# The second MLP product of 24 of 32 hidden row tiles as Strassen's seven products, in three groups

## The reference

```python
def finish_layer(x, pool_out, attn_out, w_out, ln2, w_ff1, w_ff2):
    h = x + jnp.einsum('bte,ed->btd', jnp.concatenate([pool_out, attn_out], axis=-1), w_out)
    a = jnp.square(jax.nn.relu(jnp.einsum('btd,df->btf', rmsnorm(h, ln2), w_ff1)))
    return h + jnp.einsum('btf,fd->btd', a, w_ff2)
```

## Time and profile before

| | us |
|---|---|
| median of three runs | 1344.92 |
| the profiled execution: span from first to last instruction | 1342.0 |
| up product, Strassen part (669.70 to 952.18) | 282.48 |
| down, group 0 (952.18 to 998.60) | 46.42 |
| down, groups 1 to 6 (998.60 to 1278.50) | 279.90 |
| last group and final norm (1278.50 to 1342.0) | 63.50 |

### The profile page before, as it was taken

The page is one execution under the profiler, slowest core; times in us unless marked ns, Lnnn a source line. Parts: engine busy times, 40 slices in busy tenths (PEclk is TensorE's granted clock), DMA queues, the critical chain, the costliest instruction groups (busy, mean ns, idle before and its releaser), DMA issues.

```text
span 1342.0 us, 25249 instructions
## 1 busy us (share of the span) xinstructions
PE 1308.6 (98%) x9720; PEld 1213.7 (90%) x9720; DVE 695.1 (52%) x1613; ACT 533.7 (40%) x1077; POOL 583.8 (44%) x607
## 2 busy tenths in 40 slices
PE   5999999999999999999999999999999999999998
PEld 4959999995667899779999999999999999999997
DVE  6368998759974222137843443433634334433445
ACT  6445888638766222235533333333310110011034
POOL 5434984432330312221476767767333333333610
PEclk9999999999999999999999999999999999999999
DMA  6430124210010966872332332323521333133203
GB/s 194 93 90 16 48 56 123 86 32 1 2 33 17 325 209 190 269 238 80 104 128 89 121 104 97 120 94 110 206 100 45 112 113 112 47 113 112 63 1 130
DMA packets 143550, 141.69 MB, mean 106 GB/s; under 512 B 21080, under 2 KB 111320, under 8 KB 143423
## 3 DMA queue, kind: packets, MB, share of 16 engines
q1 hardware_dynamic: 124933, 116.31, 27.3%
q10 hardware_dynamic: 17842, 21.94, 4.5%
q0 software_dynamic: 656, 1.84, 0.6%
HBM read 111.87 MB, written 26.50 MB: 103 GB/s over the span
## 4 chain that ended last, share of the span: by engine, by line
PE 84%; DVE 4%; ACT 2%; issue 1%; DMA 0%; SPq 0%; DVEq 0%; ACTq 0%
PE bank L2102 77%; PE bank L2293 3%; PE bank L2392 2%; DVE junk L1675 1%; PE bank L2347 1%; ACT sjunk L1123 1%; PE bank L2150 1%; DVE cc_lo L1755 0%; DVE hid_lo L2027 0%; PE bank L2634 0%; DVE lack L1679 0%; PE bank L2319 0%; DVE prob L1768 0%; DVE hn_lo L1903 0%; ACT prob L1215 0%
## 5 line engine op out<-in xcount | busy, mean ns | idle before, releaser
L2102 PE MATMUL bank<-hid_hi,w_hi 128*128 128x384 f32 (+1 forms) x672 | 217.6, 324 | 0.0
L2102 PE MATMUL bank<-hid_lo,w_hi 128*128 128x384 f32 (+1 forms) x672 | 216.1, 324 | 0.8 <-DVE hid_lo L2027 0.8
L2102 PE MATMUL bank<-hid_hi,w_lo 128*128 128x384 f32 (+1 forms) x672 | 216.2, 322 | 0.0
L2059 DVE TENSOR_TENSOR acc<-bank,acc 128x384 f32<-128x384 f32 x168 | 87.7, 524 | 199.3 <-PE bank L2102 199.3
L693 POOL TENSOR_TENSOR w_hi<-w_raw,zero 128x256 fp32r<-128x256 f32 x108 | 68.5, 634 | 202.3 <-PE bank L2102 186.0
L907 POOL TENSOR_TENSOR w_hi<-w_raw,zero 128x1024 fp32r<-128x1024 f32 x29 | 54.9, 1893 | 221.3 <-PE bank L2102 203.4
L2102 PE MATMUL bank<-xn_hi,w_hi 128*128 128x384 f32 (+1 forms) x456 | 150.6, 330 | 0.0
L2102 PE MATMUL bank<-xn_lo,w_hi 128*128 128x384 f32 (+1 forms) x456 | 147.3, 323 | 0.0
L2102 PE MATMUL bank<-xn_hi,w_lo 128*128 128x384 f32 (+1 forms) x456 | 146.9, 322 | 0.0
L1420 ACT ACTIVATE hid_hi<-hraw 128x1056 fp32r<-128x1056 f32 x32 | 32.7, 1077 | 256.2 <-PE bank L2102 167.1
L2102 PE MATMUL bank<-hi_T,hn_hi 128*128 128x264 f32 x448 | 127.5, 285 | 0.0
(11 more groups left out here) (300 smaller groups left out, 3213.0 us busy)
## 6 DMA issues: line engine op xcount, KB each, us to landing
w_raw<-in_w_ff_dram SPq DMA_DIRECT2D x50, 512.0 KB, 3.5
hraw<-hidden_dram SPq DMA_DIRECT2D x16, 1056.0 KB, 7.5
page<-in_cache_k_dram SPq DMA_DIRECT2D x64, 256.0 KB, 3.6
page<-in_cache_v_dram SPq DMA_DIRECT2D x64, 256.0 KB, 3.4
hidden_dram<-stg ACTq DMA_DIRECT2D x56, 264.0 KB, 2.0
w_raw<-in_w_in_dram SPq DMA_DIRECT2D x18, 512.0 KB, 3.6
wr<-in_w_ff_dram SPq DMA_DIRECT2D x14, 512.0 KB, 4.6
xrow<-in_x_prompt_dram SPq DMA_DIRECT2D x8, 512.0 KB, 8.1
```

Source lines behind the costliest of these rows:

```text
L2059: nc.vector.tensor_tensor(v, ps[:, 0:w], v, ALU.add).then_inc(freeof(("dn", gi, m, g)), 1)
L2102: return nc.tensor.matmul(out, lhsT, rhs, start=start, stop=stop)
```

## The change

Groups 0 and 7 stay as they are. The 24 hidden tiles between them, groups 1 to 6, become SG = 3 groups of eight tiles. In each, the product (1024 output features x 1024 hidden rows) by (1024 hidden rows x 1056 tokens) is cut in half in all three directions: `a11`, `a12`, `a21`, `a22` are quarters of the weights (first index: half of the output features, second: half of the hidden rows; 4 x 512 = 2048 elements per partition), `b11` to `b22` quarters of the hidden rows (first index: half of the rows, second: half of the tokens; 4 x 528 = 2112 elements). Seven products are formed, in the order P1, P2, P5, P3, P6, P7, P4, each of four row blocks by two runs of 264 columns by four tiles of K by three matmuls, 96 matmuls in all.

For each product ScalarE copies the a operand and then the b operand to `ao_hi` and `bo_hi` (two slots each, so a copy waits for the product before the last), GpSimd subtracts to get `ao_lo`, VectorE to get `bo_lo`. In place, GpSimd forms four sums of the a quarters and VectorE four of the b quarters in each group. SP loads the quarters, each as soon as its place has been used for the last time.

The products are summed over the three groups: P2 to P5 go straight into quarters of `acc`, P1, P6 and P7 into SBUF tiles of their own. Only in the third group, between its products, does VectorE combine them (`combine_parts`, 8 kinds x 4 row blocks, 528 elements each). The low half of the last hidden rows (`last_low`) is formed within the third group's P4, and the last weights are loaded to places of their own and split by ScalarE and GpSimd at the end of it.

```diff
+    KH = 4
+    SG = (DFF // P - 2 * FG) // (2 * KH)
+    DPRODS = ["P1", "P2", "P5", "P3", "P6", "P7", "P4"]
+    NQ = 7 * SG
+    MP = KC // 2
+    NCF = 8 * MP
...
+        b_q = {n: at(n, A_X + j * BQ, [P, KH, HT], F) for j, n in enumerate(("b11", "b21", "b12", "b22"))}
+        a_q = {n: at(n, o, [P, KH, MP * P], F) for n, o in (("a11", A_X + 6 * BQ), ("a22", A_X + 6 * BQ + AQ),
+                                                          ("a12", A_V + 2 * HS), ("a21", A_V + 2 * HS + AQ))}
...
+        bo_hi = [at(f"bo_hi{i}", o, [P, KH, HT], R) for i, o in enumerate((A_X + 4 * BQ, A_V))]
+        bo_lo = [at(f"bo_lo{i}", o + BQ, [P, KH, HT], R) for i, o in enumerate((A_X + 4 * BQ, A_V))]
+        ao_hi = [at(f"ao_hi{i}", o, [P, KH, MP * P], R) for i, o in enumerate((A_O0, A_O1))]
+        ao_lo = [at(f"ao_lo{i}", o + AQ, [P, KH, MP * P], R) for i, o in enumerate((A_O0, A_O1))]
...
+        for q in range(NQ):
+            for i in range(MP):
+                for h in range(2):
+                    take(("ds", q, i, h), 2 * ((MP * q + i + 3) % 4) + h)
...
+            def a_load(sg, n):
+                m, h = int(n[1]) - 1, int(n[2]) - 1
+                f0 = FG + 2 * KH * sg + KH * h
+                sp.dma_start(a_q[n][:, :, :], wf2k[:, f0:f0 + KH, MP * P * m:MP * P * (m + 1)]).then_inc(s_qa[n], 16)
+
+            def b_load(sg, n):
+                h, t = int(n[1]) - 1, int(n[2]) - 1
+                f0 = FG + 2 * KH * sg + KH * h
+                sp.dma_start(b_q[n][:, :, :],
+                             hid_d[f0:f0 + KH, :, HT * t:HT * (t + 1)].rearrange("k p t -> p k t")).then_inc(s_qb[n], 16)
...
-            for gi in range(NG):
-                for i in range(FG):
-                    down_load(gi, i, N_FF + FG + FG * gi, 0)
-                    if gi == 0 and i == 1:
-                        hidden_load(0)
-                    if i == 2 and gi + 1 < NG:
-                        hidden_load(gi + 1)
...
+                    stored_upto(FG + 2 * KH)
+                    for s in range(2):
+                        wait_full(sp, ("P3", NPR - 1, s))
+                    b_load(0, "b11")
+                    a_load(0, "a11")
+            b_load(0, "b12")
+            b_load(0, "b21")
+            a_load(0, "a22")
+            sp.wait_ge(s_fl, FG)
+            a_load(0, "a12")
+            a_load(0, "a21")
+            b_load(0, "b22")
+            for sg in range(1, SG):
+                q0 = 7 * (sg - 1)
+                stored_upto(FG + 2 * KH * (sg + 1))
+                sp.wait_ge(s_dbs, 4 * (sg - 1) + 2)
+                b_load(sg, "b12")
+                sp.wait_ge(s_dal, q0 + 4)
+                a_load(sg, "a12")
+                sp.wait_ge(s_dal, q0 + 5)
+                sp.wait_ge(s_das, 4 * (sg - 1) + 4)
+                a_load(sg, "a21")
+                sp.wait_ge(s_dbl, q0 + 5)
+                sp.wait_ge(s_dbs, 4 * (sg - 1) + 4)
+                b_load(sg, "b22")
+                sp.wait_ge(s_dal, q0 + 6)
+                a_load(sg, "a11")
+                sp.wait_ge(s_dbl, q0 + 6)
+                b_load(sg, "b11")
+                sp.wait_ge(s_dbl, q0 + 7)
+                b_load(sg, "b21")
+                sp.wait_ge(s_dal, q0 + 7)
+                a_load(sg, "a22")
...
+            sp.wait_ge(s_dbs, 4 * (SG - 1) + 2)
+            hidden_in(hlast, DFF // P - FG, 0, s_hd[2])
+            sp.wait_ge(s_dal, q0 + 4)
+            for i in range(2):
+                sp.dma_start(wl_raw[i][:, :].rearrange("p (k n) -> p k n", k=FG), wf2[NG - 1, i]).then_inc(s_lw, 16)
+            sp.wait_ge(s_dal, q0 + 5)
+            sp.wait_ge(s_das, 4 * (SG - 1) + 4)
+            for i in range(2, FG):
+                sp.dma_start(wl_raw[i][:, :].rearrange("p (k n) -> p k n", k=FG), wf2[NG - 1, i]).then_inc(s_lw, 16)
+            sp.wait_ge(s_dbl, q0 + 5)
+            sp.wait_ge(s_dbs, 4 * (SG - 1) + 4)
+            hidden_in(hlast, DFF // P - FG, 2, s_hd[3])
...
+            def a_low(q, n):
+                pool.wait_ge(s_dah, q + 1)
+                nc.gpsimd.tensor_tensor(ao_lo[q % 2][:, :, :], a_q[n][:, :, :], ao_hi[q % 2][:, :, :].bitcast(F),
+                                        ALU.subtract).then_inc(s_dal, 1)
+
+            def a_sum(dst, x, y, op):
+                nc.gpsimd.tensor_tensor(a_q[dst][:, :, :], a_q[x][:, :, :], a_q[y][:, :, :], op).then_inc(s_das, 1)
+
+            for sg in range(SG):
+                q0 = 7 * sg
+                a_low(q0, "a11")
+                a_low(q0 + 1, "a12")
+                pool.wait_ge(s_qa["a21"], Q_LOADED + 16 * (sg + 1))
+                pool.wait_ge(s_qa["a22"], Q_LOADED + 16 * (sg + 1))
+                a_sum("a21", "a21", "a22", ALU.add)
+                a_low(q0 + 2, "a21")
+                pool.wait_ge(s_das, 4 * sg + 1)
+                pool.wait_ge(s_dal, q0 + 3)
+                a_sum("a21", "a21", "a11", ALU.subtract)
+                pool.wait_ge(s_das, 4 * sg + 2)
+                a_sum("a12", "a12", "a21", ALU.subtract)
+                a_low(q0 + 3, "a12")
+                a_sum("a11", "a22", "a21", ALU.subtract)
+                a_low(q0 + 4, "a21")
+                a_low(q0 + 5, "a11")
+                a_low(q0 + 6, "a22")
+            for i in range(FG):
+                pool.wait_ge(s_wha, len(act_high) + i + 1)
+                nc.gpsimd.tensor_tensor(wl_lo[i][:, :], wl_raw[i][:, :], wl_hi[i][:, :].bitcast(F),
                                         ALU.subtract).then_inc(s_wlo, 1)
-            wait_full(pool, ("dn", NG - 2, KC - 1, 2))
+            pool.wait_ge(s_cf, NCF)
...
+            def product_high(q):
+
+                sg, name = q // 7, DPRODS[q % 7]
+                if q == 0:
                     act.wait_ge(s_fl, FG)
+                elif q == 1:
+                    wait_full(act, ("dn", 0, KC - 1, 2))
                 else:
-                    wait_full(act, ("dn", gi - 2, KC - 1, 2))
-                for k in ks:
-                    act.wait_ge(s_hd[2 * slot + k // 2], 16 * (gi // 2 + 1))
-                    nc.scalar.activation(hid_hi[slot][:, k, :], src[:, k, :], ACT.Copy).then_inc(s_hh, 1)
+                    wait_full(act, ("ds", q - 2, MP - 1, 1))
+                a, a_steps = {"P1": ("a11", 0), "P2": ("a12", 0), "P5": ("a21", 1), "P3": ("a12", 3), "P6": ("a21", 2),
+                              "P7": ("a11", 4), "P4": ("a22", 0)}[name]
+                b, b_steps = {"P1": ("b11", 0), "P2": ("b21", 0), "P5": ("b12", 1), "P3": ("b22", 0), "P6": ("b22", 2),
+                              "P7": ("b11", 3), "P4": ("b21", 4)}[name]
+                if a_steps:
+                    act.wait_ge(s_das, 4 * sg + a_steps)
+                else:
+                    act.wait_ge(s_qa[a], Q_LOADED + 16 * (sg + 1))
+                nc.scalar.activation(ao_hi[q % 2][:, :, :], a_q[a][:, :, :], ACT.Copy).then_inc(s_dah, 1)
+                if b_steps:
+                    act.wait_ge(s_dbs, 4 * sg + b_steps)
+                else:
+                    act.wait_ge(s_qb[b], Q_LOADED + 16 * (sg + 1))
+                nc.scalar.activation(bo_hi[q % 2][:, :, :], b_q[b][:, :, :], ACT.Copy).then_inc(s_dbh, 1)
...
+            def last_weight_high(i):
+
+                act.wait_ge(s_lw, 16 * FG)
+                act.wait_ge(s_dal, NQ)
+                if i >= 2:
+                    wait_full(act, ("ds", NQ - 2, MP - 1, 1))
+                nc.scalar.activation(wl_hi[i][:, :], wl_raw[i][:, :], ACT.Copy).then_inc(s_wha, 1)
...
+            for q in range(NQ):
+                product_high(q)
+            last_weight_high(0)
+            last_weight_high(1)
+            for k in range(FG):
+                wait_full(act, ("ds", NQ - 2, MP - 1, 1))
+                act.wait_ge(s_hd[2 + k // 2], 16)
+                nc.scalar.activation(hl_hi[:, k, :], hlast[:, k, :], ACT.Copy).then_inc(s_hh, 1)
+            last_weight_high(2)
+            last_weight_high(3)
...
+            def last_low(k):
+
+                dve.wait_ge(s_dbl, NQ)
+                dve.wait_ge(s_hh, FG + k + 1)
+                nc.vector.tensor_tensor(hl_lo[:, k, :], hlast[:, k, :], hl_hi[:, k, :].bitcast(F),
+                                        ALU.subtract).then_inc(s_fl, 1)
+
+            def product_low(q):
+
+                b = {"P1": "b11", "P2": "b21", "P5": "b12", "P3": "b22", "P6": "b22", "P7": "b11", "P4": "b21"}[DPRODS[q % 7]]
+                dve.wait_ge(s_dbh, q + 1)
+                nc.vector.tensor_tensor(bo_lo[q % 2][:, :, :], b_q[b][:, :, :], bo_hi[q % 2][:, :, :].bitcast(F),
+                                        ALU.subtract).then_inc(s_dbl, 1)
+
+            def b_sum(sg, dst, x, y, op, steps, lows):
+
+                if steps:
+                    dve.wait_ge(s_dbs, 4 * sg + steps)
+                dve.wait_ge(s_dbl, 7 * sg + lows)
+                nc.vector.tensor_tensor(b_q[dst][:, :, :], b_q[x][:, :, :], b_q[y][:, :, :], op).then_inc(s_dbs, 1)
...
+            def combine_parts(dst, x, y, op, i, needs=0):
+
+                if needs:
```

(82 more changed lines are left out.)

200 lines of the change are left out of this document (106 added, 94 removed).

## The result

The kernel before takes 1344.17 us (median of four runs, 1343.24 to 1348.1), the changed one 1368.18 us (four runs, 1365.83 to 1370.81): 24.0 us more, ratio 1.0171 with a 95% interval of 1.0150 to 1.0193. It is slower. 1371 was forecast, with a range of 1344 to 1392.

What follows compares the result with a forecast made beforehand. TensorE's matmul stream was taken to bound the kernel. Groups of 2 x 92.6 + 116 = 301.2 us for 279.9 give +21.3, with the clock +26: span 1368, plus 2.9 to the shown time, 1371 us; range 1344 to 1392.

Steps and rivals of the forecast that it cites:

- Matmuls: TensorE in the replaced stretch: 2016 matmuls at 121.3 ns replace 279.9 us, so TensorE alone gains 35.4 us.
- Durations: Operations per product, extrapolated from nearest rows: ScalarE 1.90 and 1.95 us, GpSimd 4.59 us, VectorE 2.36 us.
- The steady group: Each of the first two new groups: stalls before P3 and P6 make it 92.6 us, 11.0 over its 81.5.
- The Trainium skill's rule: VectorE and GpSimd's shared SBUF ports: an exclusive lock for a whole instruction, also against VectorE instructions with two SBUF inputs.
- The last group: Third new group: combining steps taking turns with GpSimd and a late last low half make it 116 us, 34.5 over.
- The walk: Following the engines' turns through the new groups: 92.6 us for each steady group, 116 for the last.
- the clock: TensorE's clock drops after pauses, before P6 and ahead of the last tiles: 5 us lost, bounds 0 and 12.
- the last group adds 32 combining steps: Third new group: 32 steps on VectorE, 528 elements from two SBUF tiles, 0.70 us each, taking turns with GpSimd.
- The loads, the longer DMAs and the earlier wait for `lnf`: Edits around the new groups, claimed at no cost; loads a few us once if their cover were gone.
- The path isn't the limit: Rival for the new groups: only P4's row blocks, the last low half and one clock drop remain; 1315 us, chance 0.12.
- The last group does no worse: Rival: third group stalls like the steady ones plus 4 us at its end; 1349 or 1340 us, chance 0.12.

Runs made afterwards that it cites:

- e1: Changed kernel with combining steps on one column and VectorE's b low halves and b sums taking their second operand from PSUM, values wrong: 1317.92 us.
- e5: Changed kernel with VectorE's low halves before b sums in P3 and P6, three combining steps in group 0, two a sums moved to VectorE, GpSimd's last later: 1342.08 us.
- e2: Changed kernel with the combining steps working on one column rather than 528: 1344.45 us.
- e6: e5 with 20 combining steps moved into the last stage, four behind P7, and the last low halves ahead of P4's additions: 1321.45 us.
- e7: Changed kernel with three of the four combining steps ahead of the first new group done within group 0: 1367.23 us.

## Why the prediction was right, step by step

- Matmuls: 121.3 ns forecast, 121.4 measured. The part removed is 278.7 us rather than 279.9, because the cuts at 998.60 and 1278.50 lie 1.5 and 0.4 us ahead of the true first matmuls. TensorE alone gains 34.0 us, not 35.4. e1, with pauses of 3.1 and 4.0 us left, is 26.0 us below the kernel before.
- Durations: GpSimd 4.59 forecast, 4.62 measured when alone; VectorE 2.36 and 2.35; ScalarE 1.90 and 1.95 forecast, 1.92 and 1.95 measured. The straight lines drawn through two sizes held at twice the larger one.
- The steady group: P3 at 41.2 us after the group's start, measured 40.6 and 40.9; P6 at 57.6, measured 56.2 in the second group; length 92.6, measured 91.2. The order of turns in the second group was as followed, and all of the 1.4 us less lies ahead of P6, a little in most of its turns. e1 shows that the turns are the cause, e5 that 82.6 us are to be had with 4.5 us less on the path ahead of P3 and VectorE's order changed.
- The Trainium skill's rule (SBUF — State Buffer, SBUF: two separate sides) had been seen up to 2.4 us; the trace of after and e1 agree with it for instructions of 4.6 us.
- The last group: P6 at 66.7, measured 64.8; P4 at 99, measured 96.5; the end at 116, measured 114.0. e2 and e6 show that the combining steps are what sets it apart: 97 us with one column each, 90 with most of them moved and the order of e5. The walk, which leaves out the clock, was 3.5 us too long here (116 forecast; 114.0 measured, of which 1.5 is the clock).
- A step that failed: "the last group adds 32 combining steps". The walk itself placed 28, as the code has them; the other four stand ahead of the first group (the description of the change overlooks them as well), and the sum gave them no cost. There they make P2 9.2 us late. Most of it comes back, since GpSimd uses the pause for its sums and P3 is then in time: that group is 94.0 us where the second is 91.2, so the term left out is 2.8 us. e7 takes that pause away and gets the one at P3 in its place: 92.7 us, and 91.2 without the 1.55 of its clock.
- A term that was mis-sized in the profiled execution: the clock, forecast at +5 us, cost 1.5. The mechanism is there. TensorE alone in three windows of after, in the third group where P6 and P4 begin, and where the last stage begins (columns as for e7 above):

```profile
1251.00:1253.00 2.00, 1.35 (x6) 0.50 0.00 0
...
1284.00:1286.00 2.00, 2.00 (x11) 0.50 0.00 0
...
1300.00:1302.00 2.00, 1.03 (x6) 1.00 0.00 0
```

  After the pauses of 10.7 and 6.9 us TensorE works at the lower level (0.50, 1.2 GHz) for 3.4 and 5.8 us, and so it does behind the pauses before P2 of the first group and P3 of the others. What that costs can be read mostly by setting after beside e7, whose code is the same from the second group on, but whose clock fell at other places:
  - At P2 of the first group next to nothing: P2 takes 1.8 us longer, but P5's operand is ready only 0.2 us before P5 starts.
  - At P3 nothing, as forecast: in the second group it takes 14.5 us in after and 13.1 in e7, and P6 starts 56.1 us after the group's start in both. VectorE, which makes P6's operand, is held meanwhile by additions and by a turn with GpSimd.
  - At P6 all of it: there the clock falls in e7 and not in after, and the group is 1.6 us longer, as P6 is. In the third group P6 takes 13.3 us in after and 14.2 in e7, and P4 and the end of the group come 0.9 us later.
  - At P4 nothing: it takes 14.3 us in after and 13.4 in e7, and from its start to the last stage it is 17.6 us in both. VectorE's first block there is held by a turn until 1288.9 us.
  - Where the last stage begins, 1.4 us: in e7 the clock reads 0.50 there, in after 1.00.

  The forecast charged P6 of all three groups and the start of the last stage, which are the right places. In after's profiled execution it fell at one of them, in e7's at all four, where it cost about 7 us. So the term isn't wrong in kind, but it changes from execution to execution. That the total came within 3 us of the forecast is in part chance: of the 26.3 us forecast, 2.3 too many are the walk's and the matmuls' and 3.5 the clock's; in their place stand 1.6 us by which the second product begins later and 2.1 us by which the medians differ more than the profiled runs (24.0 to 21.9). A clock that fell more often in the other executions would do the latter, which is not shown.
- The loads, the longer DMAs and the earlier wait for `lnf` cost nothing, as forecast: no wait of TensorE in this stretch ends with a DMA, and the last stage is as long as before.
- The rivals. "The path isn't the limit" gave 1315: e1 reaches 1318 once the path is taken away, so its number is near right for a kernel that doesn't share the path, with the reserve that e1 also leaves out the combining steps' 22 us of work. "The last group does no worse" gave 1340 to 1349, which is e2's 1344.45: in the full kernel it would have needed the combining steps to find GpSimd idle. That is what e6 gives them.

## What to carry to other kernels

When work is moved from TensorE to the engines around it, add up how long GpSimd and VectorE's instructions with two SBUF operands need their common path, not each engine's busy time, and follow the turns through one period by hand: at 76.5 of 81.5 us, with dependencies, 9.6 us were lost per group. The cures were to give that work to the engine that does it in half the time, to put the low half that is wanted next ahead of sums wanted later, and to move short steps to where the other engine is idle; cutting the long operations made it worse, since it lengthened the work on the path and cut the side that was waited for. Short instructions suffer most: four steps of 0.7 us took 11.4.
